# Attention outputs kept in HBM as plain rows of channels instead of blocks of a token tile

## The chip, the cores and the metric

The kernel runs on one core of a Trainium2 chip. Its metric is the device time of one execution in microseconds. All arithmetic is in 32-bit floats; the matrix products split each operand in a high and a low part and add three products, so that TensorE, fed with the parts, gives back nearly the full 32-bit result.

## The reference

One layer of a streaming encoder, for 2048 tokens of width 1024. A normed input is projected; the columns feed two groups of eight heads (head width 64): attention in a short window, with a learned sink (`swa`), and causal attention with a forget bias (`fox`). Their outputs are concatenated, head after head, to 1024 channels, multiplied by `w_out`, added to the input, and a feed-forward part follows.

```python
h = rmsnorm(x, norm_mix[l])
proj = jnp.einsum('bsd,de->bse', h, w_in[l])
...
out_a = swa_sink_attention(qa, ka, va, sinks[l])      # 8 heads x 64
out_b = forgetting_attention(qb, kb, vb, f_logit)     # 8 heads x 64
mixed = jnp.concatenate([out_a, out_b], axis=-1)
x = x + jnp.einsum('bse,ed->bsd', mixed, w_out[l])
h = rmsnorm(x, norm_mlp[l])
u = jax.nn.relu(jnp.einsum('bsd,df->bsf', h, w_up[l]))
x = x + jnp.einsum('bsf,fd->bsd', u * u, w_down[l])
return rmsnorm(x, norm_final)
```

## The kernel before

Four stages run one after the other, each a block with a program for every engine, joined by semaphores; between two stages all engines meet. Tile names begin with the letter of the stage.

- `project` (`p_`, to about 418 us): norm, transpose, projection. Results go to HBM.
- `attend` (`a_`, to about 1119 us): a loop over 8 pairs of heads (one `swa`, one `fox` head, both called h). In a turn the weighted values of 512 queries are summed in one PSUM bank (`a_ps_o`), ScalarE copies the bank to one of four buffers (`a_o`, line 957), and SyncE stores it: rows 0 to 63 (the main part) to `o_main`, rows 64 to 127 (the part from the low halves) to `o_rest`. A turn has eight such banks. The copy waits until the store of four banks earlier has landed. The outputs aren't divided by the softmax sums yet: the inverses go to HBM too, as `rsum_inv`.
- `mix_out` (`m_`, to about 1355 us): 16 tiles of 128 tokens, two buffer slots, a pair of tiles per turn. For a tile SyncE loads `m_mix`, `m_rest` and `m_inv` (the inverses, spread over the 64 partitions of a head, hence two DMAs), GpSimd adds the first two (line 1166), VectorE multiplies by the third (line 1228), ScalarE and VectorE split the result in a high and a low part (lines 1192 and 1232), and TensorE multiplies with the split `w_out` (line 1303: 48 products of 128x512 a tile). The sum is added to `x` (line 1262), stored as `x_mid`, normed, transposed and split to `h_hi`, `h_lo`. Those of the first eight tiles are also stored to HBM, a pair at a time (line 1125), after the second, third, fourth and fifth pair has begun.
- `mlp` (`f_`, to the end).

Every DMA is issued by SyncE (`SPq` in the rows), which works its list in order, and in this trace the DMAs move their data in the order in which they were issued. In `mix_out` its list begins with the loads of tile 0, then `w_out` (4 MB in all), two constants, the loads of tile 1, two tiles of `x` and a part of `w_up`. After that, per tile: the mix loads of the tile two ahead (once its slot's split is done), the wait for line 1262, the `x_mid` store, the next `x` load, and in slot 0 of the second to fifth pair the two `h` stores of 1 MB each.

The layout is what this case is about. The scratch tensors are made in `hybrid_block`; `store_outputs` (line 622) writes `o_main` and `o_rest`, and `load_mix` (line 1099) reads them. Before, `o_main` has the shape (16 token tiles, 128, 8 heads, 128 tokens), where the 128 is 64 channels of `swa` over 64 of `fox`. A load of a tile so finds 8 x 128 floats, 4096 bytes, in one run for each partition; a store of 512 tokens of a head breaks in runs of 512 bytes, four for each channel. Since partition p then holds channels of two heads k of different kinds, the rows of `w_out` for chunk k come from two places, and each chunk is loaded by two DMAs of 64 partitions.

Of the kernel before, what the change touches and what calls it, by code (L numbers as in the profile page):

```python
# [388 lines left out]
def attend(nc, proj_hi, proj_lo, sinks, ident_dram, causal_dram, alibi_dram,  # L389
# [68 lines left out]
    with ExitStack() as ctx:  # L458
# [119 lines left out]
        @block.sync  # L578
        def _(sp):
            def load(dst, src, done):  # L580
                sp.dma_start(dst, src).then_inc(done, 16)


            def load_qk(kind, q0, k0, done, cols=slice(0, S)):
                for part, half in ((0, proj_hi), (1, proj_lo)):
                    rows = slice(part * DH, (part + 1) * DH)
                    load(q_st[kind][rows, cols].bitcast(F32), half[bass.ds(P + q0, DH), cols], done)
                    for dst, src in ((k_hi, proj_hi), (k_lo, proj_lo)):
                        load(dst[kind][rows, cols].bitcast(F32), src[bass.ds(P + k0, DH), cols], done)

            def load_v(kind, v0):
                for part, half in ((0, proj_hi), (1, proj_lo)):
                    load(v_t[kind][part * DH:(part + 1) * DH], half[bass.ds(P + v0, DH), :], v_loaded[kind])

            def load_bias(h, done):
                load(alibi[:], alibi_dram[bass.ds(h, 1)].rearrange("a p c -> (a p) c"), done)
                load(sink[:], sinks[0, bass.ds(h, 1)].partition_broadcast(P), done)

            def load_swa(h):
                load_qk("swa", h * DH, KA + (h // GROUP) * DH, qk_loaded["swa"])  # L600
                load_bias(h, qk_loaded["swa"])
                load_v("swa", VA + (h // GROUP) * DH)

            def load_fox(h):
                load_qk("fox", QF + h * DH, KF + h * DH, qk_loaded["fox"])
                load(decay_sb[:], decay[bass.ds(h, 1)].rearrange("a s -> (a s)").partition_broadcast(P),
                     qk_loaded["fox"])
                load_v("fox", VF + h * DH)

            for done in (*o_stored, r_stored):  # L610
                sp.sem_inc(done, 16)

            load_qk("swa", 0, KA, first_loaded, slice(0, S // 2))
            load_bias(0, first_loaded)
            sp.sem_inc(qk_loaded["swa"], 32)
            load_qk("swa", 0, KA, qk_loaded["swa"], slice(S // 2, S))
            load(ident[:], ident_dram, const_in)
            load(causal[:], causal_dram, const_in)
            load_v("swa", VA)
            load_fox(0)  # L620

            def store_outputs(h, n):
                sp.wait_ge(o_copied, h * O_BLOCKS + (n + 3))
                kind, b = divmod(n, QB)
                for part, dst in ((0, o_main), (1, o_rest)):
                    load(dst[4 * b:4 * b + 4, kind * DH:(kind + 1) * DH, bass.ds(h, 1)].rearrange("t d a s -> d t (a s)"),
                         o_sb[n % O_RING][part * DH:(part + 1) * DH].rearrange("d (t s) -> d t s", s=P),
                         o_stored[n % O_RING])

            def turn(h, last=False):  # L630
                if not last:

                    sp.wait_ge(scored, chunk_count(h, ("swa", QT // 2 - 1)))
                    sp.wait_ge(v_done["swa"], 4 * (h + 1))
                    sp.wait_ge(sink_exped, h + 1)
                    load_swa(h + 1)
                for n in range(QB + 2):
                    store_outputs(h, n)
                if not last:

                    sp.wait_ge(scored, chunk_count(h, ("fox", 3, 3, 3)))
                    sp.wait_ge(v_done["fox"], 4 * (h + 1))
                    load_fox(h + 1)
                store_outputs(h, QB + 2)
                sp.wait_ge(r_copied, h + 2)
                for part in range(2):
                    load(rsum_inv[:, part, bass.ds(h, 1)].rearrange("t a q -> t (a q)"),
                         recip_t[part * QT:(part + 1) * QT], r_stored)
                store_outputs(h, QB + 3)

            with sp.Fori(0, H - 1) as h:
                turn(h)
            turn(H - 1, True)
            for done in o_stored:
                sp.wait_ge(done, 16 + 32 * H * O_BLOCKS // O_RING)
            sp.wait_ge(r_stored, 16 + 32 * H)
# [352 lines left out]
def mix_out(nc, o_main, o_rest, rsum_inv, w_out, x, norm_mlp, w_up, ident_dram, h_hi, h_lo, wu_raw,  # L1009
# [7 lines left out]

    S, D = x.shape  # L1020
    ST, EK, DK = S // P, SWA_HEADS, D // P
    HALVES = D // BANK
    PAIRS = ST // 2
    KEPT = MLP_TOKENS // P
# [2 lines left out]
    with ExitStack() as ctx:  # L1027
# [70 lines left out]
        def _(sp):  # L1098
            def load_mix(pair, slot):
                t = 2 * pair + slot  # L1100
                if not in_first_pair(pair):
                    sp.wait_ge(mix_lo_done, t - 1)
                    sp.nop(nofuse=True)
                done = o_loaded[slot]
                for dst, src in ((mix, o_main), (rest, o_rest)):
                    sp.dma_start(dst[:, slot], src[bass.ds(t, 1)].rearrange("a p k s -> (a p) k s")).then_inc(done, 16)
                for kind in range(2):
                    rows = slice(kind * HEAD_DIM, (kind + 1) * HEAD_DIM)
                    src = rsum_inv[bass.ds(t, 1), kind].rearrange("a k s -> (a k) s")
                    sp.dma_start(inv[rows, slot], src.partition_broadcast(HEAD_DIM)).then_inc(done, 16)  # L1110

            def load_x(pair, slot):
# [14 lines left out]

            load_mix(0, 0)
            for k in range(EK):
                for kind in range(2):  # L1130
                    row = (kind * SWA_HEADS + k) * HEAD_DIM
                    sp.dma_start(w_raw[k][kind * HEAD_DIM:(kind + 1) * HEAD_DIM],
                                 w_out[row:row + HEAD_DIM, :]).then_inc(w_loaded[k], 16)
            sp.dma_start(ident[:], ident_dram).then_inc(const_in, 16)
            sp.dma_start(gain[:], norm_mlp[0].partition_broadcast(P)).then_inc(const_in, 16)
            load_mix(0, 1)
# [48 lines left out]
        @block.scalar  # L1185
        def _(act):
            def split_mix(pair, slot):
                t = 2 * pair + slot
                act.wait_ge(divided, t + 1)
                if not in_first_pair(pair):  # L1190
                    act.wait_ge(summed, HALVES * (t - 1))
                nc.scalar.activation(mix_hi[:, slot], mix[:, slot], ACT.Copy).then_inc(mix_hi_done, 1)

            def split_ht(pair, slot, at):
                t = 2 * pair + slot
                if isinstance(pair, int) and (pair, slot) == (BLOCK, 0):
                    act.wait_ge(ht_stored, 32 * BLOCK)
                for half in range(2):
                    act.wait_ge(turned, 2 * t + half + 1)
                    nc.scalar.activation(h_hi[:, 4 * half:4 * half + 4, bass.ds(at, P)],  # L1200
                                         ps_t[2 * slot + half][:].rearrange("p (k s) -> p k s", s=P),
                                         ACT.Copy).then_inc(ht_hi_done, 1)

            split_mix(0, 0)
            for k in range(EK):
                act.wait_ge(w_loaded[k], 32)
                nc.scalar.activation(w_hi[:, k], w_raw[k], ACT.Copy).then_inc(w_hi_done, 1)

            def tile(pair, slot, at, first_block):
                t = 2 * pair + slot  # L1210
                if not is_last(pair, slot):
                    split_mix(pair + slot, 1 - slot)
                act.wait_ge(added, 2 * t + 2)
                if not in_first_pair(pair):
                    act.wait_ge(turned, 2 * (t - 1))
                nc.scalar.activation(xn[:, slot], xm[:, slot], ACT.Square,
                                     accum_out=ssum[:, slot:slot + 1]).then_inc(squared, 1)
                if not is_first(pair, slot):
                    split_ht(pair - 1 + slot, 1 - slot, at)

            walk(act, tile)
            split_ht(PAIRS - 1, 1, (KEPT - 1) * P)
# [444 lines left out]
def hybrid_block(nc, x, norm_mix, w_in, b_forget, sinks, w_out, norm_mlp, w_up, w_down, norm_final,  # L1667
# [2 lines left out]
    x, out = (a.rearrange("b s d -> (b s) d") for a in (x, out))  # L1670
    w_in, w_out, w_up, w_down = (w.rearrange("l a b -> (l a) b") for w in (w_in, w_out, w_up, w_down))
    S, D = x.shape
    rows = -(-w_in.shape[1] // P) * P

    def scratch(name, *shape):
# [1 line left out]

    proj_hi, proj_lo = scratch("proj_hi", rows, S), scratch("proj_lo", rows, S)
    decay = scratch("decay", FOX_HEADS, S)
    o_main, o_rest = (scratch(name, S // P, P, SWA_HEADS, P) for name in ("o_main", "o_rest"))  # L1680
    rsum_inv = scratch("rsum_inv", S // P, 2, SWA_HEADS, P)
    x_mid = scratch("x_mid", S, D)
    h_hi, h_lo = scratch("h_hi", D, S), scratch("h_lo", D, S)

# [26 lines left out]
```

## Time and profile before

| | us |
|---|---|
| three runs | 2800.79, 2803.12, 2803.32 (median 2803.12) |
| the profiled execution's own time | 2800.79 |
| its span on the core | 2799.0 |
| TensorE busy | 2616.7 (93%) |
| VectorE busy | 1397.3 (50%) |
| ScalarE busy | 924.7 (33%) |
| GpSimd busy | 75.9 (3%) |
| share of the 16 DMA engines | 36.7% |

The span runs from the first to the last instruction; 1.8 us of the time lie around it. Busy is the time in which an engine had an instruction in work. The DMA share is an average, and it is far from even: in slices of 70 us it goes from 0% to 80%, and the part between 1120 and 1290 us is the fullest.

### The profile page before, as it was taken

The numbers are of one execution on the slowest core, as the hardware profiler recorded it, in microseconds if no ns is written. First come the engines' busy times: TensorE is split into PE (matmuls) and PEld (weight loads), VectorE is DVE, ScalarE is ACT, GpSimd is POOL, SyncE is SP. The second block draws the span as 40 slices with busy tenths as digits, with TensorE's granted clock in tenths as the row PEclk, the third lists the DMA queues.
The fourth block names the chain that finished last, engine by engine and source line by source line (L and its number), as shares of the span: only waits on it lengthen the run. The fifth ranks groups of instructions, "written<-read, shape, count | busy, mean of one in ns | idle before, by whom it ended". The sixth has DMA issues, their size and how long they took to land.

```text
span 2799.0 us, 35983 instructions
## 1 busy us (share of the span) xinstructions
PE 2616.7 (93%) x12624; PEld 2163.2 (77%) x12624; DVE 1397.3 (50%) x2476; ACT 924.7 (33%) x1669; POOL 75.9 (3%) x116
## 2 busy tenths in 40 slices
PE   7999996788988889599899999999999999999997
PEld 6788885677877778487788888888878888888886
DVE  6311111577777777456344444444454444444445
ACT  5211112577777777222212121121222121121211
POOL 2000000000000000122000000000000000000000
PEclk9999998899999999799999999999999999999999
DMA  4333335577656762897311010110271011110101
GB/s 159 143 112 112 122 133 150 138 163 167 143 140 140 163 139 60 245 301 247 131 43 60 30 60 30 60 60 30 80 251 61 31 60 48 42 60 30 60 31 75
DMA packets 151161, 301.43 MB, mean 108 GB/s; under 512 B 10776, under 2 KB 105752, under 8 KB 137624
## 3 DMA queue, kind: packets, MB, share of 16 engines
q1 hardware_dynamic: 151072, 300.39, 36.7%
q8 instruction: 37, 0.61, 0.1%
q14 instruction: 52, 0.43, 0.0%
HBM read 218.37 MB, written 81.99 MB: 107 GB/s over the span
## 4 chain that ended last, share of the span: by engine, by line
PE 50%; DVE 0%; ACT 0%; DMA 0%; POOL 0%; issue 0%; ACTq 0%; POOLq 0%
PE f_ps_u L1621 26%; PE f_ps_d L1636 25%; DMA out<-f_y 0%; DVE f_y L1569 0%; DVE f_wd_lo L1546 0%; ACT f_wd_hi L1488 0%; ACT f_y L1507 0%; POOL f_rstd L1468 0%; DVE f_wu_lo L1541 0%; ACT f_wu_hi L1482 0%; DVE f_acc L1564 0%; POOL f_rstd L1465 0%; ACTq L1333 0%; POOLq L1461 0%; POOLq L1464 0%
## 5 line engine op out<-in xcount | busy, mean ns | idle before, releaser
L1564 DVE TENSOR_TENSOR f_acc<-f_acc,f_ps_d 128x512 f32<-128x512 f32 x512 | 343.5, 686 | 223.2 <-PE f_ps_d L1636 223.2
L1621 PE MATMUL f_ps_u<-h_hi_kept,f_wu_hi 128*128 128x512 f32 x1024 | 406.5, 397 | 4.0 <-DVE f_wu_lo L1541 4.0
L1636 PE MATMUL f_ps_d<-f_wd_hi,f_u_hi 128*128 128x512 f32 x1024 | 401.3, 392 | 8.8 <-DVE f_wd_lo L1546 8.8
L1621 PE MATMUL f_ps_u<-h_lo_kept,f_wu_hi 128*128 128x512 f32 x1024 | 406.2, 397 | 0.0
L1621 PE MATMUL f_ps_u<-h_hi_kept,f_wu_lo 128*128 128x512 f32 x1024 | 406.1, 397 | 0.0
L1636 PE MATMUL f_ps_d<-f_wd_lo,f_u_hi 128*128 128x512 f32 x1024 | 401.0, 392 | 0.0
L1636 PE MATMUL f_ps_d<-f_wd_hi,f_u_lo 128*128 128x512 f32 x1024 | 400.3, 391 | 0.0
L1496 ACT ACTIVATE f_r<-f_ps_u 128x512 f32<-128x512 f32 x128 | 76.5, 597 | 959.2 <-PE f_ps_u L1621 959.2
L861 DVE TENSOR_TENSOR a_pt_lo<-a_ps_t,a_pt_hi 128x512 fp32r<-128x512 f32 (+3 forms) x384 | 234.8, 618 | 139.5 <-ACT a_pt_hi L950 137.1
L1555 DVE TENSOR_TENSOR f_sq<-f_r 128x512 f32<-128x512 f32 x128 | 88.6, 692 | 396.4 <-ACT f_r L1496 394.8
L950 ACT ACTIVATE a_pt_hi<-a_ps_t 128x512 fp32r<-128x512 f32 (+3 forms) x384 | 204.3, 542 | 113.1 <-PE a_ps_t L750 65.1
L352 PE MATMUL p_ps_o<-p_ht_hi,p_w_hi 128*128 128x512 f32 x608 | 238.6, 392 | 3.0 <-DVE p_w_lo L270 3.0
L352 PE MATMUL p_ps_o<-p_ht_lo,p_w_hi 128*128 128x512 f32 x608 | 237.6, 391 | 0.0
L352 PE MATMUL p_ps_o<-p_ht_hi,p_w_lo 128*128 128x512 f32 x608 | 237.4, 391 | 0.0
L1636 PEld LDWEIGHTS f_ps_d<-f_wd_hi,f_u_hi 128*128 128x128 f32 x1024 | 193.5, 189 | 50.5 <-DVE f_wd_lo L1546 9.6
L1621 PEld LDWEIGHTS f_ps_u<-h_hi_kept,f_wu_hi 128*128 128x128 f32 x1024 | 193.1, 189 | 51.0 <-DVE f_wu_lo L1541 4.4
L1621 PEld LDWEIGHTS f_ps_u<-h_hi_kept,f_wu_lo 128*128 128x128 f32 x1024 | 193.0, 188 | 46.8
L1621 PEld LDWEIGHTS f_ps_u<-h_lo_kept,f_wu_hi 128*128 128x128 f32 x1024 | 193.1, 189 | 46.4
L1636 PEld LDWEIGHTS f_ps_d<-f_wd_hi,f_u_lo 128*128 128x128 f32 x1024 | 193.6, 189 | 40.7
L1636 PEld LDWEIGHTS f_ps_d<-f_wd_lo,f_u_hi 128*128 128x128 f32 x1024 | 193.5, 189 | 40.4
L279 DVE TENSOR_TENSOR p_o_lo<-p_ps_o,p_o_hi 128x512 fp32r<-128x512 f32 x76 | 52.5, 692 | 303.4 <-ACT p_o_hi L211 303.4
L780 PE MATMUL a_ps_o<-a_pt_hi,a_v_fox 128*128 128x512 f32 (+1 forms) x320 | 147.1, 460 | 48.0 <-DVE a_pt_lo L861 47.8
(122 smaller groups left out, 3862.2 us busy)
## 6 DMA issues: line engine op xcount, KB each, us to landing
wu_raw_kept<-in_w_up SPq DMA_DIRECT2D x32, 1024.0 KB, 7.3
f_wd_raw<-in_w_down SPq DMA_DIRECT2D x32, 1024.0 KB, 5.0
proj_hi<-p_o_hi SPq DMA_DIRECT2D x18, 1024.0 KB, 4.0
proj_lo<-p_o_lo SPq DMA_DIRECT2D x18, 1024.0 KB, 6.7
p_w_raw<-in_w_in SPq DMA_DIRECT2D x19, 512.0 KB, 7.8
p_x_in<-in_x SPq DMA_DIRECT2D x16, 512.0 KB, 4.1
a_k_hi_fox<-proj_hi SPq DMA_DIRECT2D x16, 512.0 KB, 12.0
a_k_lo_fox<-proj_lo SPq DMA_DIRECT2D x16, 512.0 KB, 13.7
```

The source lines that it names most:

```text
L279: nc.vector.tensor_tensor(o_lo[:, slot, s], ps_o[bank][:], o_hi[:, slot, s].bitcast(F32), ALU.subtract).then_inc(o_lo_done, 1)
L352: last = nc.tensor.matmul(ps_o[bank][:], w[:, slot, k, :], h[:, k, s], start=(k == 0 and n == 0), stop=(k == DK - 1 and n == 2))
L780: last = nc.tensor.matmul(bank[:, BANK - w:BANK], v_st[kind][:, step[2]], pt[:, 0:w], start=(first and pt is hi), stop=(last_one and pt is ...
L861: nc.vector.tensor_tensor(pt_lo[i % PT_RING][:, lo:hi], bank[:, lo:hi], pt_hi[i % PT_RING][:, lo:hi].bitcast(F32), ALU.subtract).then_inc( ...
L950: nc.scalar.activation(pt_hi[i % PT_RING][:, lo:hi], bank[:, lo:hi], ACT.Copy).then_inc(p_hi_done, 1)
L1496: nc.scalar.activation(r[:, n % 2], ps_u[n][:], ACT.Relu).then_inc(relu_done, 1)
L1555: nc.vector.tensor_tensor(sq[:, n % 2], r[:, n % 2], r[:, n % 2], ALU.mult).then_inc(sq_done, 1)
L1564: nc.vector.tensor_tensor(acc[:, t, cols], acc[:, t, cols], ps_d[n % RING][:], ALU.add).then_inc(added, 1)
L1621: last = nc.tensor.matmul(ps_u[n][:], w[:, k, f * P:(f + 1) * P], h[:, k, s * BANK:(s + 1) * BANK], start=(k == 0 and m == 0), stop=(k == ...
L1636: last = nc.tensor.matmul(ps_d[n % RING][:], u[parity][:, f, t * P:(t + 1) * P], w[:, f, half * BANK:(half + 1) * BANK], start=(f == 0 and ...
```

## The change

Three scratch tensors get another shape: `o_main` and `o_rest` become (1024 channels, 2048 tokens), and `rsum_inv` (16 heads, 2048 tokens), with the channels in the order of the reference. A store now has 64 runs of 2048 bytes, and a load of a tile of `o_main` or `o_rest` 8 runs of 512 bytes in each of 128 partitions; a load of inverses has 8 runs of 512 bytes for each of 64 partitions, where it was one run of 4096. Chunk k of the channels is now 128 adjacent rows of `w_out`, loaded by one DMA of 128 partitions.

```diff
             def store_outputs(h, n):
                 sp.wait_ge(o_copied, h * O_BLOCKS + (n + 3))
-                kind, b = divmod(n, QB)
+                row = (n // QB) * KA + h * DH
+                cols = slice((n % QB) * BANK, (n % QB + 1) * BANK)
                 for part, dst in ((0, o_main), (1, o_rest)):
-                    load(dst[4 * b:4 * b + 4, kind * DH:(kind + 1) * DH, bass.ds(h, 1)].rearrange("t d a s -> d t (a s)"),
-                         o_sb[n % O_RING][part * DH:(part + 1) * DH].rearrange("d (t s) -> d t s", s=P),
-                         o_stored[n % O_RING])
+                    load(dst[bass.ds(row, DH), cols], o_sb[n % O_RING][part * DH:(part + 1) * DH], o_stored[n % O_RING])
...
                 for part in range(2):
-                    load(rsum_inv[:, part, bass.ds(h, 1)].rearrange("t a q -> t (a q)"),
+                    load(rsum_inv[bass.ds(part * H + h, 1)].rearrange("a (t q) -> (a t) q", q=P),
                          recip_t[part * QT:(part + 1) * QT], r_stored)
...
             def load_mix(pair, slot):
                 t = 2 * pair + slot
+                s = bass.ds(t * P, P)
...
-                for dst, src in ((mix, o_main), (rest, o_rest)):
-                    sp.dma_start(dst[:, slot], src[bass.ds(t, 1)].rearrange("a p k s -> (a p) k s")).then_inc(done, 16)
-                for kind in range(2):
-                    rows = slice(kind * HEAD_DIM, (kind + 1) * HEAD_DIM)
-                    src = rsum_inv[bass.ds(t, 1), kind].rearrange("a k s -> (a k) s")
+                sp.dma_start(mix[:, slot], o_main[:, s].rearrange("(k p) s -> p k s", p=P)).then_inc(done, 16)
+                sp.dma_start(rest[:, slot], o_rest[:, s].rearrange("(k p) s -> p k s", p=P)).then_inc(done, 16)
+                for half in range(2):
+                    rows = slice(half * HEAD_DIM, (half + 1) * HEAD_DIM)
+                    src = rsum_inv[:, s].rearrange("(k two) s -> two k s", two=2)[half]
                     sp.dma_start(inv[rows, slot], src.partition_broadcast(HEAD_DIM)).then_inc(done, 16)
...
             for k in range(EK):
-                for kind in range(2):
-                    row = (kind * SWA_HEADS + k) * HEAD_DIM
-                    sp.dma_start(w_raw[k][kind * HEAD_DIM:(kind + 1) * HEAD_DIM],
-                                 w_out[row:row + HEAD_DIM, :]).then_inc(w_loaded[k], 16)
+                sp.dma_start(w_raw[k], w_out[k * P:(k + 1) * P, :]).then_inc(w_loaded[k], 16)
...
             for k in range(EK):
-                act.wait_ge(w_loaded[k], 32)
+                act.wait_ge(w_loaded[k], 16)
                 nc.scalar.activation(w_hi[:, k], w_raw[k], ACT.Copy).then_inc(w_hi_done, 1)
...
-    o_main, o_rest = (scratch(name, S // P, P, SWA_HEADS, P) for name in ("o_main", "o_rest"))
-    rsum_inv = scratch("rsum_inv", S // P, 2, SWA_HEADS, P)
+    o_main, o_rest = scratch("o_main", E, S), scratch("o_rest", E, S)
+    rsum_inv = scratch("rsum_inv", SWA_HEADS + FOX_HEADS, S)
```

TensorE, VectorE, ScalarE and GpSimd keep their instructions in the same order; only SyncE's list changes. At the start of `mix_out` it stands so before, where `m_x_in`, `m_xm`, `m_xn` and `wu_raw_kept` are the buffers that first hold `w_out`:

```order
L1106 DMA m_mix<-o_main 128x1024
L1106 DMA m_rest<-o_rest 128x1024
L1110 DMA m_inv<-rsum_inv 64x1024 x2
L1132 DMA m_x_in<-in_w_out 64x1024 x4
L1132 DMA m_xm<-in_w_out 64x1024 x4
L1132 DMA m_xn<-in_w_out 64x1024 x4
L1132 DMA wu_raw_kept<-in_w_out 64x1024 x4
L1134 DMA m_ident<-in_ident 128x128
L1135 DMA m_gain<-in_norm_mlp 128x1024
```

And now:

```order
L1106 DMA m_mix<-o_main 128x8x128
L1107 DMA m_rest<-o_rest 128x8x128
L1112 DMA m_inv<-rsum_inv 64x8x128 x2
L1132 DMA m_x_in<-in_w_out 128x1024 x2
L1132 DMA m_xm<-in_w_out 128x1024 x2
L1132 DMA m_xn<-in_w_out 128x1024 x2
L1132 DMA wu_raw_kept<-in_w_out 128x1024 x2
L1133 DMA m_ident<-in_ident 128x128
L1134 DMA m_gain<-in_norm_mlp 128x1024
```

The mix loads carry as many bytes as before in eight times the runs, and sixteen loads of `w_out` over 64 partitions become eight over 128; nothing changes its place. In a turn of `attend` SyncE's stores behind the loads of the next head stand so before (the next line of each is its wait for the next bank):

```order
L581 DMA a_v_t_swa<-proj_lo 64x2048
L623 ISA
L581 ISA
L581 DMA o_main<-a_o 64x4x128
L581 DMA o_rest<-a_o 64x4x128
```

And now:

```order
L581 DMA a_v_t_swa<-proj_lo 64x2048
L623 ISA
L581 ISA
L581 DMA o_main<-a_o 64x512
L581 DMA o_rest<-a_o 64x512
```

Only the shape of the two stores differs: four runs of 128 floats for each partition became one of 512.

## Rows read from the trace of the kernel before

**Rows 1.** The page, busy time, share of the span and instructions:

```profile
PE 2616.7 (93%) x12624; PEld 2163.2 (77%) x12624; DVE 1397.3 (50%) x2476; ACT 924.7 (33%) x1669; POOL 75.9 (3%) x116
```

**Rows 2.** Waits, 1119 to 1400: waiter, releaser, total us, times, longest:

```profile
PE m_ps_o L1303 <- DVE m_w_lo L1249: 20.0, 2, 19.7
PE m_ps_o L1303 <- DVE m_mix_lo L1232: 13.3, 4, 9.3
```

**Rows 3.** Timeline at the start of mix_out: start, duration, instruction, idle before it:

```profile
1123.58 0.38 SPq L1106 DMA_DIRECT2D m_mix<-o_main  x1
...
1131.77 2.34 POOL L1166 TENSOR_TENSOR m_mix<-m_mix,m_rest 128x1024 f32<-128x1024 f32 x1 [1071.38 <-DMA m_inv<-rsum_inv]
...
1138.99 0.77 PE L1303 MATMUL m_ps_o<-m_w_hi,m_mix_hi 128*128 128x512 f32 x1 [19.73 <-DVE m_w_lo L1249]
...
1152.96 0.40 PE L1303 MATMUL m_ps_o<-m_w_hi,m_mix_lo 128*128 128x512 f32 x1
...
1156.53 2.34 POOL L1166 TENSOR_TENSOR m_mix<-m_mix,m_rest 128x1024 f32<-128x1024 f32 x1 [22.42 <-DMA m_inv<-rsum_inv]
...
1162.62 0.77 PE L1303 MATMUL m_ps_o<-m_w_hi,m_mix_hi 128*128 128x512 f32 x1 [9.26 <-DVE m_mix_lo L1232]
```

**Rows 4.** Windows there: stretch, length, busy times, granted clock, DMA share, GB/s:

```profile
1131.00:1147.00 16.00, 8.01 (x24) 6.37 (x25) 9.23 (x8) 7.18 (x7) 2.34 (x1) 0.57 1.04 238
1150.00:1152.00 2.00, 1.73 (x8) 1.15 (x7) 1.23 (x1) 0.39 (x1) 0.00 (x0) 1.00 1.04 414
1154.00:1156.00 2.00, 0.00 (x0) 0.00 (x0) 0.00 (x0) 0.00 (x0) 0.00 (x0) 1.00 1.02 211
1158.00:1160.00 2.00, 0.00 (x0) 0.00 (x0) 1.10 (x1) 0.00 (x0) 0.86 (x1) 0.58 1.09 353
1168.00:1170.00 2.00, 2.00 (x9) 1.65 (x8) 0.37 (x1) 0.00 (x0) 1.60 (x1) 0.86 1.03 416
```

**Rows 5.** Windows in project, a load of w_in in 512-byte runs, 128 partitions:

```profile
222.00:224.00 2.00, 2.00 (x11) 1.65 (x10) 1.55 (x2) 0.55 (x1) 0.00 (x0) 1.00 0.93 259
224.00:226.00 2.00, 2.00 (x10) 1.67 (x9) 0.00 (x0) 0.00 (x0) 0.00 (x0) 1.00 0.67 200
```

**Rows 6.** Timeline of GpSimd in mix_out, the additions of tiles 5, 7, 9, 13, 15:

```profile
1206.54 2.40 POOL L1166 TENSOR_TENSOR m_mix<-m_mix,m_rest 128x1024 f32<-128x1024 f32 x1 [3.55 <-DMA m_inv<-rsum_inv]
...
1231.62 2.39 POOL L1166 TENSOR_TENSOR m_mix<-m_mix,m_rest 128x1024 f32<-128x1024 f32 x1 [4.79 <-DMA m_inv<-rsum_inv]
...
1256.96 2.39 POOL L1166 TENSOR_TENSOR m_mix<-m_mix,m_rest 128x1024 f32<-128x1024 f32 x1 [5.07 <-DMA m_inv<-rsum_inv]
...
1302.35 2.40 POOL L1166 TENSOR_TENSOR m_mix<-m_mix,m_rest 128x1024 f32<-128x1024 f32 x1
...
1325.91 2.40 POOL L1166 TENSOR_TENSOR m_mix<-m_mix,m_rest 128x1024 f32<-128x1024 f32 x1
```

**Rows 7.** Timeline of TensorE, the start of tile 7:

```profile
1237.83 0.49 PE L1303 MATMUL m_ps_o<-m_w_hi,m_mix_hi 128*128 128x512 f32 x1 [1.24 <-DVE m_mix_lo L1232]
```

**Rows 8.** Windows in the turn of tiles 8 to 10:

```profile
1243.00:1249.00 6.00, 6.00 (x29) 4.94 (x28) 4.56 (x4) 1.06 (x1) 0.52 (x1) 1.00 1.01 325
1262.00:1264.00 2.00, 0.98 (x4) 0.83 (x5) 2.00 (x3) 0.00 (x0) 0.00 (x0) 1.00 0.38 82
```

**Rows 9.** Timeline of a turn of attend: a stall on a store, and after it:

```profile
694.47 0.60 ACT L957 ACTIVATE a_o<-a_ps_o 128x512 f32<-128x512 f32 x1 [6.77 <-DMA o_rest<-a_o]
...
696.34 0.79 PE L780 MATMUL a_ps_o<-a_pt_hi,a_v_fox 128*128 128x512 f32 x1 [5.63 <-DVE a_pt_lo L861]
```

**Rows 10.** Waits, 500 to 1115, ScalarE's for the stores:

```profile
ACT a_o L957 <- DMA o_rest<-a_o: 47.6, 7, 7.0
```

**Rows 11.** Windows in attend: queued stores, a lone store, the clock after the stall:

```profile
693.00:694.00 1.00, 0.00 (x0) 0.00 (x0) 0.00 (x0) 0.00 (x0) 0.00 (x0) 1.00 1.15 322
695.00:696.00 1.00, 0.00 (x0) 0.00 (x0) 0.41 (x1) 1.00 (x3) 0.00 (x0) 0.50 1.04 307
709.00:710.00 1.00, 1.00 (x8) 0.89 (x7) 0.87 (x3) 1.00 (x1) 0.00 (x0) 1.00 0.80 186
```

More of the change, by code:

```diff
@@ L1010, in mix_out @@
             x_mid, h_hi_dram, h_lo_dram):
-    S, D = x.shape
-    ST, EK, DK = S // P, SWA_HEADS, D // P
+    E, S = o_main.shape
+    D = w_out.shape[1]
+    EK, DK, ST = E // P, D // P, S // P
     HALVES = D // BANK
@@ L1672, in hybrid_block @@
     S, D = x.shape
+    E = w_out.shape[0]
     rows = -(-w_in.shape[1] // P) * P
```

## The prediction, made before the changed kernel was run

> **What bounds the kernel now.** I read the busy times first: TensorE works 93% of the span [rows 1], so a change to DMAs can only count where TensorE waits for one. The change touches SyncE's list alone, in two places: the stores in `attend` and the start and steady part of `mix_out`. So I read the waits of the second stage next. From 1119 to 1400 us TensorE's large waits are two: 20.0 us for the split of `w_out`, nearly all of it (19.7) at the start, and 13.3 us in four times for the split of the mix [rows 2]. The timeline says where: TensorE begins at 1138.99, ends tile 0 at 1152.96 + 0.40 = 1153.36, and waits 9.26 us for tile 1; its mix is added on GpSimd at 1156.53, when the last DMA of tile 1 has landed, and 6.09 us later, at 1162.62, TensorE starts [rows 3]. The windows then say what the DMAs did: from 1131 to 1147 they were busy without a gap (share 1.04) and moved 238 GB/s, and at 1150 they moved 414 GB/s at the same share [rows 4]. The first are the loads of `w_out` over 64 partitions, the second loads over 128. So a DMA that touches 64 partitions runs at 0.57 of the rate here; loads of inverses, also over 64, show 211 [rows 4].
>
> In the steady part three of GpSimd's additions wait for a load, 25.08 and 25.34 us apart [rows 6], where two tiles without such a wait take 1325.91 - 1302.35 = 23.56 us [rows 6]. So from tile 5 to tile 11 the DMAs set the pace, by a loop: `h` stores, mix loads, addition, products, `x_mid` store, next `h` stores. TensorE waits 1.24 us for tile 7 [rows 7]; with the 9.26 taken from the 13.3, the other two, for tiles 9 and 11, come to 2.8. For tile 5 it doesn't wait, and has 0.28 us to spare: the loop's 25.08 less TensorE's 23.56 for two tiles less the 1.24 that it waits at tile 7.
>
> **The change part by part.**
>
> *Mix and rest loads.* 1 MiB (1.049 MB) a tile. Before, at 414 GB/s over a share of 1.04 [rows 4], 398 to 414: I take 410, so 2.56 us. After, runs of 512 bytes over 128 partitions. The load of `w_in` has just that shape, and moves 200 / 0.67 = 299 and 259 / 0.93 = 278 GB/s [rows 5]. So 3.51 to 3.77 us: 0.95 to 1.21 more; I take 1.05.
>
> *Inverse loads.* 0.524 MB a tile over 64 partitions, 2.2 us at 238 GB/s [rows 4]. No row shows loads of 512-byte runs to 64 partitions, but a lone store of them from 64 does 186 / 0.80 = 233 GB/s [rows 11], the rate of the long runs over 64. By that the half of the partitions bounds both, and the loss is 0. If the loss of 512-byte runs over 128 partitions came on top, it were half of 0.95, about 0.5. I take 0.2, near the row that is most alike. So a tile costs d = 1.25 us of DMA time more, between 0.95 and 1.7.
>
> *`w_out`.* 4.194 MB at 238 GB/s are 17.6 us; at 410 they are 10.2. It saves 7.4 us of DMA time (bounds: 414 and 398 GB/s after, 7.5 and 7.1). Its issues aren't the limit before, since the share is full.
>
> *The start.* TensorE's first product waits for tile 0's mix and then for the first chunk of `w_out`: it comes d = 1.25 later, at 1140.2, and tile 0, whose products take 14.4 us, ends at 1154.6 (the chunks now arrive faster than TensorE takes them). Before tile 1's addition lie two tiles' mix loads and all of `w_out`: 2d - 7.4 = -4.9 us. So TensorE starts tile 1 at 1157.7 and waits 3.1 instead of 9.26. Tiles 1 to 4 follow with TensorE's pace: their loads come d later than the shift, and the additions of tiles 3 and 4 don't wait before.
>
> *The clock.* In that wait of 9.26 us the granted clock falls to the lower level, 1.2 GHz (mean 0.58 from 1158 to 1160), and is back by 1168 to 1170 (0.86) [rows 4]: about 6 us of tile 1 at half speed, 3 us lost. A wait of 5.63 us in `attend` ends in it too [rows 9, 11]. For a wait of 3.1 us there is no row; 1.24 us [rows 7] does nothing. If the clock holds, tile 2 becomes the limit (its loads come only 3d - 7.4 = -3.65 earlier), and of the 3 us some 1.8 are gained. I take half of it, -0.9; bounds 0 and -1.8.
>
> *The loop.* For each of tiles 5, 7, 9 and 11 the mix load stands between the `h` stores and the addition, so the loop grows by d. Tile 5 has 0.28 of slack: 0.97; the other three 1.25 each: +4.7 in sum. The load of the even tile stands in the same turn, but before the `x_mid` store, where the DMAs have a gap: at 1262 to 1264 their share is 0.38 [rows 8], 1.2 us idle, so its 1.25 just fits. The addition of that tile has more room than that before TensorE needs it. Later tiles have no `h` stores and loads to spare.
>
> *The stores in `attend`.* ScalarE waits 47.6 us in seven turns for a store [rows 10], and TensorE stands for 5.63 us behind it [rows 9]: this is on the path. But the time goes in the loads of the next head, which lie ahead of the store and don't change; only the store's own 0.262 MB count. Before, queued stores run at 322 / 1.15 = 280 GB/s [rows 11], 0.94 us. After, with runs of 2048 bytes, between the 64-partition rate of 233 (1.13 us) and 410 (0.64): +0.2 to -0.3 in each of seven turns. I take 0; bounds +1.3 and -2.1. The last store before `mix_out` goes the same way: 0.
>
> Sum: -4.9 - 0.9 + 4.7 = -1.1 us. Against the profiled execution's 2800.79 (its span of 2799.0 and 1.8 around it) that is 2799.7; the median of the runs before is 2.3 higher, by which it would be 2802.0. I say 2801. In d the sum without the clock is 6d - 7.7: 0 at 1.28, -5.6 at 0.35, +5.6 at 2.2.
>
> A rule of the Trainium skill would give another d. "DMA: Bandwidth & Descriptors", section "Why small descriptors are slow (HBM only)", says that each packet costs about 3 fixed beats beside one for each 32 bytes. An estimate from that page: 512 bytes at 16/19 of 435 GB/s, so 366, and 4096 at 425; d would be 0.4 and the sum -5.3. The trace shows a larger loss, 278 to 299 GB/s against 414 [rows 4, 5], so I don't go by the rule.
>
> **The rivals.**
>
> *A. Short runs cost more than on the row of `w_in`, and the loads of `mix_out` become its limit.* The place is `load_mix`, the price d. Where inverse loads lose too, and mixed with stores the short runs fall to some 230 GB/s (4.56 us, 2.0 more, + 0.5), d is 2.5: 6 x 2.5 - 7.7 = +7.3, and the even tile no longer fits its gap (1.25 over 1.2, in three turns, +3.9, partly hidden): +7 to +11, 2810. It decides from d = 2.2 on. For it speaks that DMA shares are near 1 from 1243 to 1249 [rows 8] and that no row shows this load; against it that `w_in` is the same shape.
>
> *B. The rows of the new tensors, 8 KB apart, with steps of 1 MB between the eight runs, slow the reads as such.* At half the rate, 150 GB/s, d is 3.5 + 0.95 = 4.4, and the sum 6 x 4.4 - 7.7 = +19; 2820. Against it: the `h` stores, 1024-byte runs at the same spacing, move 325 GB/s [rows 8]. The Trainium skill has such a rule for pitches of large powers of two ("DMA: Bandwidth & Descriptors", "Latency and other measured facts"), measured at longer runs; no row here shows it.
>
> *C. Faster by more than can be measured.* d at its lower end (0.95: -2.0), the clock holds at tile 1 (-1.8), the wider stores free ScalarE sooner (-2.1): -5.9, 2795. Each has a row at one end; that all come together is the weak point.
>
> *D. The longer waits in the loop (1.3 + 1.25 = 2.6 us) drop the clock*, at 3 us a time in three or four turns: +9, 2809. Against it: it would have to happen at 2.6 us and, for the sum above, not at 3.1.
>
> **How the numbers follow.** Forecast 0.55, own range -4 to +4. A 0.17, B 0.05, C 0.18, D 0.05. What a measurement can tell from no change is about 0.2%, 5.6 us. Slower by more than that: A, B, D and little else, 0.25. Faster: most of C and an edge of the forecast, 0.2. Same: 0.55. The range leaves B out and takes in A, C and D: 2793 to 2811.
>
> **What would show it.** Right: the window of `w_out` at 400 GB/s and more; tile 1's addition some 5 us earlier against the start of the stage; additions of tiles 5 to 11 about 26.4 us apart; TensorE's waits for the mix at 2.5 us each; ScalarE's wait in `attend` within 2 us of 47.6 in all; `attend` as long as before within 2 us. Wrong: mix loads under 270 GB/s (A, B); additions of even tiles that hold TensorE up; a granted clock of 0.5 in tiles 5 to 11 (D); a wait for stores in `attend` that is gone or doubled, which would say that the stores and not the loads ahead of them were the price.

## The result, and the profile after

The changed kernel takes 2890.85 us (median of four runs, 2889.89 to 2895.11), the kernel before 2801.95 (2798.14 to 2803.32): a ratio of 1.0333, 95% interval 1.0319 to 1.0346. It is 89 us slower, where 2801 and a range of 2793 to 2811 were forecast. The profiles are of single executions (spans 2900.3 and 2799.0 us, 101.3 apart), so sums over them come out some 12 us larger than the difference of the medians.

The page of the changed kernel, which answers to [rows 1]:

```profile
PE 2640.8 (91%) x12624; PEld 2179.7 (75%) x12624; DVE 1384.7 (48%) x2476; ACT 924.7 (32%) x1669; POOL 75.4 (3%) x116
```

Its waits from 1115 to 1460 us, which answer to [rows 2] (waiter, releaser, total, times, longest):

```profile
PE m_ps_o L1302 <- DVE m_mix_lo L1231: 81.6, 15, 13.2
PE m_ps_o L1302 <- DVE m_w_lo L1248: 30.3, 1, 30.3
```

TensorE's large waits in `mix_out` grow from 33.3 to 111.9 us, by 78.6. Its busy time in the stage grows from 196.9 to 218.4 us, by 21.4, with the same instructions: they run longer at the lower clock behind those waits. Together that is 100.0, and the stage (from the first mix load's issue to the first issue of `mlp`) grew from 231.6 to 331.9 us, by 100.3. So all of the loss is there. What lies ahead of it changed by little: the stage begins 2.0 us later, and ScalarE's wait for the stores in `attend` is 47.9 us in seven times, 47.6 before [rows 10].

The timeline at the start of the stage, which answers to [rows 3] (start, duration, instruction, idle before):

```profile
1125.62 0.43 SPq L1106 DMA_DIRECT2D m_mix<-o_main  x1
...
1144.62 2.34 POOL L1165 TENSOR_TENSOR m_mix<-m_mix,m_rest 128x1024 f32<-128x1024 f32 x1 [1084.58 <-DMA m_inv<-rsum_inv]
```

```profile
1151.85 0.77 PE L1302 MATMUL m_ps_o<-m_w_hi,m_mix_hi 128*128 128x512 f32 x1 [30.32 <-DVE m_w_lo L1248]
1178.67 0.77 PE L1302 MATMUL m_ps_o<-m_w_hi,m_mix_hi 128*128 128x512 f32 x1 [13.23 <-DVE m_mix_lo L1231]
```

From the first issue to the first addition pass 19.0 us; before it was 8.2. The windows of that stretch show which load it is (stretch, length, busy times of the engines, granted clock, DMA share, GB/s):

```profile
1128.00:1130.00 2.00, 0.00 (x0) 0.00 (x0) 0.00 (x0) 0.00 (x0) 0.00 (x0) 0.50 1.17 323
...
1132.00:1134.00 2.00, 0.00 (x0) 0.00 (x0) 0.00 (x0) 0.00 (x0) 0.00 (x0) 0.50 0.10 28
1134.00:1136.00 2.00, 0.00 (x0) 0.00 (x0) 0.00 (x0) 0.00 (x0) 0.00 (x0) 0.50 0.14 45
1136.00:1138.00 2.00, 0.00 (x0) 0.00 (x0) 0.00 (x0) 0.00 (x0) 0.00 (x0) 0.50 0.13 41
```

```profile
1144.00:1150.00 6.00, 0.00 (x0) 0.00 (x0) 1.88 (x2) 1.75 (x2) 2.34 (x1) 0.50 1.03 420
1160.00:1170.00 10.00, 5.44 (x25) 4.16 (x23) 0.00 (x0) 0.00 (x0) 0.00 (x0) 1.00 0.96 36
```

The mix and rest loads come first and run at 323 GB/s; `w_out` comes last and runs at 420. Between them lie the inverse loads, at 28 to 45 GB/s, with a DMA share of 0.10 to 0.14: the engines have next to nothing in work and yet the data don't come. In tile 1 (1160 to 1170) the rate is the same, 36 GB/s, but the share is 0.96. The share is the time that packets took, and with 512 bytes a packet the windows give an estimate of one packet's time: about 30 ns in the mix loads (1128 to 1130), about the same in tile 0's inverse loads, where the time goes between packets, and about 220 ns in tile 1, where the packets themselves are slow. A DMA share near 1 doesn't say that bytes move, and one near 0 doesn't say that nothing is asked for.

In the steady stage every addition on GpSimd waits for the inverses. Its timeline, which answers to [rows 6]:

```profile
1249.42 2.34 POOL L1165 TENSOR_TENSOR m_mix<-m_mix,m_rest 128x1024 f32<-128x1024 f32 x1 [12.82 <-DMA m_inv<-rsum_inv]
...
1287.92 2.34 POOL L1165 TENSOR_TENSOR m_mix<-m_mix,m_rest 128x1024 f32<-128x1024 f32 x1 [12.39 <-DMA m_inv<-rsum_inv]
...
1414.29 2.39 POOL L1165 TENSOR_TENSOR m_mix<-m_mix,m_rest 128x1024 f32<-128x1024 f32 x1 [6.05 <-DMA m_inv<-rsum_inv]
1430.16 2.37 POOL L1165 TENSOR_TENSOR m_mix<-m_mix,m_rest 128x1024 f32<-128x1024 f32 x1 [6.42 <-DMA m_inv<-rsum_inv]
```

A pair of tiles with `h` stores takes 38.5 us (25.2 before), and even the last tiles, where before DMAs had time to spare, take 15.9 each (11.8 before).

### The profile page after: what moved, and what is told of

The parts are those of the page before. It is cut to its first block and busy times, and to the rows that moved or that the text cites. A ratio compares the mean times of both kernels' runs of the same rounds, so it can differ in the third digit from the quotient of the medians.

```text
span 2900.3 us, 35972 instructions
## 1 busy us (share of the span) xinstructions
PE 2640.8 (91%) x12624; PEld 2179.7 (75%) x12624; DVE 1384.7 (48%) x2476; ACT 924.7 (32%) x1669; POOL 75.4 (3%) x116
## 5 line engine op out<-in xcount | busy, mean ns | idle before, releaser
L1302 PE MATMUL m_ps_o<-m_w_hi,m_mix_hi 128*128 128x512 f32 x256 | 112.2, 438 | 111.9 <-DVE m_mix_lo L1231 81.6
```

The costliest lines, as they stand in the source:

```text
L1302: last = nc.tensor.matmul(ps_o[2 * slot + half][:], m[:, slot, k], w[:, k, cols], start=(k == 0 and n == 0), stop=(k == EK - 1 and n == 2))
```

## The experiments

The diffs show the part of each edit that counts (the stores of the inverses follow the layout). All times below are medians; ratios are against runs of the kernel before on the same chip.

**e1: only the inverses back in blocks.** It asks whether the short runs of the outputs share in the loss.

```diff
-rsum_inv = scratch("rsum_inv", SWA_HEADS + FOX_HEADS, S)
+rsum_inv = scratch("rsum_inv", S // P, 16, P)
...
-src = rsum_inv[:, s].rearrange("(k two) s -> two k s", two=2)[half]
+src = rsum_inv[bass.ds(t, 1), 8 * half:8 * half + 8].rearrange("a k s -> (a k) s")
```

> The changed kernel, with the inverses alone kept in blocks of a token tile (16 tiles, 16 heads in the order of the load, 128 tokens), so that an inverse load has one run of 4096 bytes for each partition again; outputs stay plain rows in 512-byte runs. Theory 1 (the whole loss is in the inverse loads, whose 64 partitions all read the same 512-byte runs): about 2801, within 6 us of before, as forecast without a cost of the inverses; the additions of tiles 5 to 11 about 26 us apart for two, the first addition about 7.5 us after the first mix load is issued plus 1. Rival (512-byte runs of the mix and rest loads carry a good part, by contention in the steady stage): at least 20 us of the 90 stay, 2820 or more.

2797.21 us, ratio 0.9986 (0.9977 to 0.9994), within the 6 us of theory 1. The whole loss is gone, and the rest of the change is a small gain. The additions of tiles 5, 7, 9 and 11 are 25.6, 27.5 and 25.6 us apart, and from first issue to first addition pass 9.2 us, 1.0 more than before.

**e2: the kernel before, with only the inverses plain.**

```diff
-src = rsum_inv[bass.ds(t, 1), kind].rearrange("a k s -> (a k) s")
+src = rsum_inv[kind * SWA_HEADS:(kind + 1) * SWA_HEADS, bass.ds(t * P, P)]
```

> The kernel before, with the inverses alone as plain rows (16 heads, 2048 tokens), loaded as 8 runs of 512 bytes, 8 KB apart, into 64 partitions; outputs and w_out as before. Theory 1: the inverse loads alone bring the whole loss and w_out's half loads stay too, so 2890 to 2905, with inverse loads at some 40 GB/s after the mix loads of tile 0. Rival (it needs both together): under 2850.

2866.6 us, ratio 1.0239 (1.0221 to 1.0257). The inverses alone do harm, but 65 us: the time lies between the two answers. The window of its first inverse loads shows a rate nearly as low as in the changed kernel's (41 GB/s from 1125 on), at twice its DMA share:

```profile
1123.00:1129.00 6.00, 0.00 (x0) 0.00 (x0) 0.00 (x0) 0.00 (x0) 0.00 (x0) 0.50 0.28 49
```

**e3: rows of the inverses 256 bytes longer.**

```diff
-rsum_inv = scratch("rsum_inv", SWA_HEADS + FOX_HEADS, S)
+rsum_inv = scratch("rsum_inv", SWA_HEADS + FOX_HEADS, S + 64)
```

> The changed kernel, with the rows of the inverses 2048 + 64 floats apart (8448 bytes) instead of 2048 (8192). Theory 2 (rows a power of two apart fall on one part of the HBM): the loss goes, 2795 to 2810. Theory 1 (the same 512-byte run is read by 64 partitions at once, whatever the spacing of the runs): 2880 to 2900 as the changed kernel.

2797.99 us, ratio 0.9995 (0.9984 to 1.0005). The same DMAs with the same shape and the same bytes, 64 readers for each run, and the loss is gone. So none of these alone makes it, not the number of runs, their length, the 64 partitions or the repeated reads. The windows in which the changed kernel crawled:

```profile
1124.00:1126.00 2.00, 0.00 (x0) 0.00 (x0) 0.00 (x0) 0.00 (x0) 0.00 (x0) 0.50 0.83 241
1126.00:1128.00 2.00, 0.00 (x0) 0.00 (x0) 0.00 (x0) 0.00 (x0) 0.00 (x0) 0.50 1.20 302
1128.00:1130.00 2.00, 0.00 (x0) 0.00 (x0) 0.00 (x0) 0.00 (x0) 0.00 (x0) 0.50 1.22 199
```

**e4: the inverse loads read 64 different rows.** The values multiplied in are rows of `o_rest`, not the inverses.

```diff
-src = rsum_inv[:, s].rearrange("(k two) s -> two k s", two=2)[half]
-sp.dma_start(inv[rows, slot], src.partition_broadcast(HEAD_DIM)).then_inc(done, 16)
+src = o_rest[:, s].rearrange("(k p) s -> p k s", p=P)[rows]
+sp.dma_start(inv[rows, slot], src).then_inc(done, 16)
```

> The changed kernel, with the inverse loads reading 64 different rows of o_rest (same bytes, same 8 runs of 512 bytes for each partition, same 64 partitions, no row read twice); the values multiplied in are so not the inverses. Theories 1 and 2 with a repeat: the loss goes, 2795 to 2810. Theory 3 (512-byte runs into 64 partitions are slow from any source): 2880 to 2900.

2796.98 us, ratio 0.9992 (0.9982 to 1.0001). Rows 8 KB apart, each read once, do no harm. The window with its inverse loads, which would have crawled:

```profile
1128.00:1130.00 2.00, 0.00 (x0) 0.00 (x0) 0.00 (x0) 0.00 (x0) 0.00 (x0) 0.50 1.25 201
```

With e3 this speaks for two conditions together: the same short run read for 64 partitions, and a certain spacing of the eight runs. The spacing is shown by e3, which changes nothing else. The repeat is less well shown, since e4 changed three things: no run is read twice, the eight runs of a partition lie 1 MB apart instead of 16 KB, and they come from another tensor, whose rows the load before has just read. No run here reads, for one partition, distinct runs 16 KB apart. The next runs ask which spacing.

**e5, e6, e7, e10: other spacings of plain rows.** e5 orders the 16 rows so that the eight of a load are adjacent; the others lengthen the rows: `2 * S`, `S + 16` and `S + 1024` in place of `S`.

> The changed kernel, with the 16 plain rows of the inverses ordered so that the 8 rows of one load are adjacent (8 KB apart) instead of every second (16 KB apart). Theory 2, refined (the spacing decides over how many parts of the HBM the 8 runs spread, so half the spacing gives more): 2845 to 2870, as e2 had it. Rival (16 KB and 8 KB are alike, and e2 was faster for another reason, its old layout of the outputs): 2885 to 2895.

> The changed kernel, with rows of the inverses 16 KB apart, so that the 8 runs of a load are 32 KB apart. Theory 2, refined: fewer parts still, over 2920. Rival (at 16 KB all runs already fall on one part): 2885 to 2895.

> The changed kernel, with rows of the inverses 2048 + 16 floats apart (64 bytes more), so that the 8 runs are shifted against each other by 128 bytes each, 896 in all, where 256 bytes more (e3) shifted them by 512 each. If a shift of less than one run's length is enough: 2795 to 2810. If the runs must lie in separate stretches of 512 bytes or more: 2840 to 2895.

> The changed kernel, with rows of the inverses 12 KB apart, so that the 8 runs of a load are 24 KB apart: no power of two, but still a multiple of 8 KB. If only the place within a stretch of 8 KB counts: 2880 to 2905, as with 8 and 16 KB. If the spacing has to be a power of two for the loss: 2795 to 2830.

**e9: short runs close together.** As e1, with 16 unused floats behind each run.

```diff
-rsum_inv = scratch("rsum_inv", S // P, 16, P)
+rsum_inv = scratch("rsum_inv", S // P, 16, P + 16)
```

> As e1 (inverses in blocks of a token tile), but with 16 unused floats behind each run, so that an inverse load is 8 runs of 512 bytes again, 576 bytes apart, all within 4.6 KB, each read by 64 partitions. Theory 4 (what counts is where the runs lie against each other; close together they are as good as one run of 4096 bytes): 2795 to 2805. Rival (it is the many requests for the same short run, wherever the next one lies): 2830 or more.

The changed kernel's line rests on four runs, those of e1, e3, e9 and e10 on eight or twelve, those of e5, e6 and e7 on two.

| kernel | from run to run, bytes | us |
|---|---|---|
| e1 | 512 (one run of 4096) | 2797.2 |
| e9 | 576 | 2798.0 |
| e5 | 8192 | 2901.5 |
| changed | 16384 | 2890.9 |
| e7 | 16512 | 2834.3 |
| e3 | 16896 | 2798.0 |
| e10 | 24576 | 2812.4 |
| e6 | 32768 | 2826.9 |

e9 came as theory 4 had it: short runs are harmless when they lie close. The refined theory 2, that a wider power of two is worse, fell on both sides: 8 KB isn't better than 16, and 32 KB is much better. That 8 KB is worse, 10 us by the medians, isn't clear: e5's ratio is 1.0340 to 1.0378, the changed kernel's 1.0319 to 1.0346. e10 lies within the answer for "only a power of two", but a loss is left: 11 us over the kernel before (ratio 1.0034, 1.0023 to 1.0046) and 15 over e1. So neither "any multiple of 8 KB" nor "only a power of two" describes it. In e7 a shift by 128 bytes from run to run, again between the two answers, takes away more than half of the loss, and in e3 one by 512 takes away all. That e7's runs no longer begin at multiples of 512 bytes isn't what is left of its loss: e9's don't either.

**e8: everything in blocks, channels in the reference's order.** Against the kernel before, `w_out`'s loads differ, and the order in which the rows of channels lie; the length of the runs is the same.

```diff
-o_main, o_rest = scratch("o_main", E, S), scratch("o_rest", E, S)
-rsum_inv = scratch("rsum_inv", SWA_HEADS + FOX_HEADS, S)
+o_main, o_rest = (scratch(name, S // P, E, P) for name in ("o_main", "o_rest"))
+rsum_inv = scratch("rsum_inv", S // P, 16, P)
...
-load(dst[bass.ds(row, DH), cols], o_sb[n % O_RING][part * DH:(part + 1) * DH], o_stored[n % O_RING])
+load(dst[4 * b:4 * b + 4, bass.ds((h % 2) * 512 + 4 * kind + h // 2, 505)][:, 0:505:8].rearrange("t d s -> d t s"),
+     o_sb[n % O_RING][part * DH:(part + 1) * DH].rearrange("d (t s) -> d t s", s=P), o_stored[n % O_RING])
...
-sp.dma_start(mix[:, slot], o_main[:, s].rearrange("(k p) s -> p k s", p=P)).then_inc(done, 16)
+sp.dma_start(mix[:, slot], o_main[bass.ds(t, 1)].rearrange("a (p k) s -> (a p) k s", k=EK)).then_inc(done, 16)
```

> Outputs and inverses all in blocks of a token tile (long runs for the loads of mix_out, as before), but with the channels in the reference's order, so that w_out is loaded by eight DMAs over 128 partitions: the kernel before with only w_out's loads changed. By the forecast's sum with d = 0: w_out's 7.4 us and up to 1.8 for the clock in tile 1, so 2791 to 2794 against 2801; and 4 to 7 us below e1. Rival (the start's gain is given back in the loop of the h stores, whose first turn then waits longer): within 2 us of before, 2799 to 2801.

2792.16 us, ratio 0.9968 (0.9956 to 0.998): 8.5 us faster than before (5.6 to 12.3 by the interval), and the fastest of all. Its windows at `w_out`'s loads and at the start of tile 1:

```profile
1136.00:1140.00 4.00, 0.00 (x0) 0.00 (x0) 2.37 (x2) 2.23 (x3) 0.48 (x1) 0.50 1.03 410
...
1158.00:1160.00 2.00, 1.89 (x8) 1.61 (x9) 1.16 (x2) 0.81 (x1) 0.00 (x0) 1.00 1.10 242
1160.00:1162.00 2.00, 2.00 (x10) 1.67 (x9) 0.57 (x1) 0.35 (x2) 0.74 (x2) 1.00 1.04 313
```

**e11 and e12: e8 with plain inverses.** e11 orders the rows as e5 does, e12 as the changed kernel. They ask why e2 lost less than e5.

> As e8 (outputs in blocks, w_out over 128 partitions), but with the inverses as plain rows, the 8 rows of one load adjacent (8 KB apart), as in e2 and e5. It asks why e2 lost 65 us and e5 100 with the same spacing. If the outputs' layout (what runs just ahead of the inverse loads) makes it: 2845 to 2865, as e2. If w_out's loads made it: 2885 to 2905, as e5.

> As e8, but with the inverses exactly as in the changed kernel (plain rows, every second one read, 16 KB apart): the inverses' part of the change on top of the best layout. If the outputs' layout matters as in e11: 2835 to 2860. If not: 2875 to 2895.

2860.89 and 2859.82 us, both as forecast for the case that the outputs' layout matters: 69 and 68 over e8. On plain outputs the same two steps cost 104 (e5 over e1) and 94 (the changed kernel over e1). So `w_out`'s loads have no part in it, and the outputs' layout has: with short runs in the mix loads the inverses cost some 30 us more. In the order "outputs, inverses" the change so splits: e8 to e1, outputs plain, +5; e8 to e12, inverses plain, +68; both, e8 to the changed kernel, +99. The traces show it already in tile 0: from the first issue to the first addition pass 9.0 us in e8 and 16.0 in e12, so the plain inverses cost 7.0 there, against 9.8 behind short runs (9.2 in e1, 19.0 in the changed kernel). Why the same loads are slower behind short runs was not settled.

## Why the prediction was wrong

*The step that failed* is "Inverse loads": "No row shows loads of 512-byte runs to 64 partitions, but a lone store of them from 64 does 186 / 0.80 = 233 GB/s [rows 11], the rate of the long runs over 64. By that the half of the partitions bounds both, and the loss is 0." I took 0.2 us a tile; in tile 0 it was 19.0 - 9.2 = 9.8 us (changed kernel against e1), and the medians, 94 us apart, make it 5.9 for each of the 16 tiles. The row was like the load in run length and in partitions, and unlike it in what the experiments point at: it moved different data for each partition, while an inverse load reads each run 64 times, the next run 16 KB away. The kernel before has such loads, but their eight runs are one stretch of 4096 bytes, at 211 GB/s [rows 4]. The range's upper bound for that term (0.5) was therefore no bound: it came from rows in which no run is read twice.

*The rivals.* A had the right place, `load_mix`, and the wrong cause and price: not short runs as such (e3, e4, e9), and not 2.5 us a tile in all but 9.8 in tile 0 for the inverses alone. (In its working, "1.25 over 1.2" should be 2.5 over 1.2, which is 1.3; the +3.9 is three of these.) B, where the rows' spacing slows the reads, came nearest to the mechanism, but I tied it to the mix and rest loads, with "half the rate": they weren't slowed (323 GB/s), and at a sixth of the rate of before the inverses were. The row of the `h` stores, 325 GB/s at the same spacing, said nothing on reads of one row by all. The rule of the Trainium skill ("DMA: Bandwidth & Descriptors", "Latency and other measured facts") is measured at pitches from 512 KiB up and on separate rows of 16 KiB. Here separate rows 8 KB and 1 MB apart show no loss (e4), and for shared ones 32 KB was better than 16. D, the clock in the loop: it did fall there, behind waits that the inverse loads had made longer, and the lower clock took 21 of the 100 us.

*What the runs showed right*, once the inverses were out of the way:

- `w_out` over 128 partitions: 410 and 420 GB/s against 238. With up to 1.8 for the clock it was to bring 7.4 to 9.2 us; e8 brings 8.5 (5.6 to 12.3).
- The clock: for a wait of 3.1 us I had no row and took half of the gain. In e8 TensorE waits 3.29 us for tile 1 and keeps the full clock, as the windows show; in e1 it waits 3.79, and the granted clock falls to 0.50, the lower level. The length of the wait doesn't decide it alone, one execution of each kernel: in e9 the clock stays at 1.00 through a wait of 3.59 us, in e1 it falls also behind one of 3.49 at tile 9 (0.53 from 1258 to 1260), and in e4 behind one of only 2.01 at tile 7 (0.50 from 1234 to 1236). So rival D's fall of the clock in the loop happens with the inverses out of the way too; in e1 it costs about 1.7 us by the windows (an estimate).
- The short runs of mix and rest: e1 over e8, 5.0 us, where 6 x 1.05 = 6.3 were counted. From tile 5 to tile 11 e1 takes 78.6 us and e8 75.3, 3.4 more for 3 x 1.05 = 3.15. The total agrees in part by luck, since e1's 5.0 also hold the two falls of the clock, at tiles 1 and 9, that e8 doesn't have.
- The sum without the inverses: 6 x 1.05 - 7.7 - 0.9 = -2.3; e1 measured -3.9 (-6.4 to -1.7 by its interval), so without the inverse loads the forecast would have held.
- The estimate from the Trainium skill for short runs ("DMA: Bandwidth & Descriptors", "Why small descriptors are slow (HBM only)"; d = 0.4) would make e1 over e8 2.4 us. The window of e1's mix loads (below) shows 305 GB/s where that estimate gives 366; the row from `project` was the better source.
- The stores in `attend`: 0 was right, and it was the loads ahead of them that ScalarE waits for.

The window with e1's mix loads, and the one behind the start of its tile 1:

```profile
1123.00:1125.00 2.00, 0.00 (x0) 0.00 (x0) 0.00 (x0) 0.00 (x0) 0.00 (x0) 0.50 1.04 305
...
1156.00:1158.00 2.00, 2.00 (x7) 1.52 (x6) 0.00 (x0) 1.01 (x2) 0.74 (x2) 0.50 1.11 252
```

The waits at tile 1 in e1 and at tile 7 in e4:

```profile
1154.77 0.47 PE L1302 MATMUL m_ps_o<-m_w_hi,m_mix_hi 128*128 128x512 f32 x1 [3.79 <-DVE m_mix_lo L1231]
...
1232.42 0.63 PE L1302 MATMUL m_ps_o<-m_w_hi,m_mix_hi 128*128 128x512 f32 x1 [2.01 <-DVE m_mix_lo L1231]
```

## What to carry to other kernels

Before a broadcast load from HBM is cut into short runs, ask how far apart they lie: 64 partitions reading the same eight 512-byte runs, 8 or 16 KB apart, were about five times slower than with one contiguous run, and the trace of the old layout can't show it. If the layout is wanted all the same, make the rows a little longer (256 bytes here), or keep together what one load reads. And a bound for an operation that no row shows is only as good as the likeness of the row: list in what it differs, here "each run is read 64 times", before calling it a bound.

## What the runs showed of the hardware that was not expected

- Eight 512-byte runs, each read for 64 partitions, 8 or 16 KB apart: about 40 GB/s. The same DMAs with 16.5 KB between the runs: 199 to 302 GB/s, the mix loads included. The time doesn't grow or fall steadily with the spacing (the table above); which rule decides is open.
- The slow reads show at about the same rate with a DMA share of 0.10 to 0.14 (28 to 45 GB/s), of 0.28 (e2) or of 0.96 (36 GB/s).
- Layouts interact: the same inverse loads cost 68 us behind mix loads in long runs (7.0 in tile 0) and 94 behind short ones (9.8).
- TensorE's granted clock fell to the lower level behind a wait of 2.01 us (e4) and stayed at the full one through a wait of 3.59 us (e9).
